# Compressed keys of the samples as weighted scores of raw pages, with page numbers kept in registers

## The reference

```python
past_cmp = kv_pool[page_table, :, 0:2].reshape(bsz, PAST_LEN, 2, NSA_KV_HEADS, NSA_HEAD_DIM)
kc, vc = nsa_compress(cmp_rows, pos_w)      # blocks of 64 rows, weighted by softmax(pos_w)
...
s_c = einsum('btkrd,bnkd->btkrn', q, kc) - slope * dist_c
p_c = masked_softmax(s_c, dist_c >= 0)
o_c = einsum('btkrn,bnkd->btkrd', p_c, vc)
imp = p_c.sum(axis=3)                       # picks the blocks of the selected branch
```

## Time and profile before

| | us |
|---|---|
| median of 3 runs | 1043.51 (1043.34 to 1045.84) |
| the profiled execution, its own time | 1046.67 |
| its span, first to last instruction | 1044.6 |
| busy in the span: TensorE, VectorE, ScalarE, GpSimd | 992.2, 492.4, 333.9, 186.0 |
| mean granted TensorE clock | 0.977 |
| loaded and stored | 343.20 MB, mean 329 GB/s |

### The profile page before, as it was taken

The page is one execution under the profiler, slowest core; times in us unless marked ns, Lnnn a source line. Parts: engine busy times, 40 slices in busy tenths (PEclk is TensorE's granted clock), DMA queues, the critical chain, the costliest instruction groups (busy, mean ns, idle before and its releaser), DMA issues. The chain is left out here.

```text
span 1044.6 us, 14969 instructions
## 1 busy us (share of the span) xinstructions
PE 992.2 (95%) x5181; PEld 618.9 (59%) x5181; DVE 492.4 (47%) x1422; ACT 333.9 (32%) x875; POOL 186.0 (18%) x201
## 2 busy tenths in 40 slices
PE   8999999899999999998999987979999999999897
PEld 6888776788744444443678864545874444444365
DVE  2889898771521111110479996671152111111056
ACT  3212888720451111110341013672045111112034
POOL 0000016321130000000345541441103000000033
PEclk9999999999999999999999995999999999999999
DMA  9963788669779999999827995959976999999974
GB/s 324 314 220 115 230 265 274 245 213 405 305 286 424 428 426 426 425 427 427 330 99 276 392 341 166 314 174 366 428 332 253 426 426 427 424 428 426 426 301 207
DMA packets 90144, 343.20 MB, mean 329 GB/s; under 512 B 15890, under 2 KB 53906, under 8 KB 73170
## 3 DMA queue, kind: packets, MB, share of 16 engines
q1 hardware_dynamic: 80074, 319.48, 78.8%
q10 hardware_dynamic: 7688, 18.39, 5.0%
q0 software_dynamic: 2304, 4.33, 1.2%
HBM read 331.56 MB, written 23.04 MB: 339 GB/s over the span
## 5 line engine op out<-in xcount | busy, mean ns | idle before, releaser
L1528 DVE TENSOR_TENSOR gates_and_hidden<-bank,gates_and_hidden 128x512 f32<-128x512 f32 x16 | 11.1, 692 | 310.6 <-PE bank L1179 310.6
L1179 PE MATMUL bank<-expert_ring,x_packed 128*64 128x512 f32 x320 | 118.3, 606 | 0.0
L1160 PE MATMUL bank<-expert_ring,x_packed 128*64 128x512 f32 x416 | 112.9, 593 | 1.1 <-DMA expert_ring<-in_moe_w_gate 0.8
L559 PE MATMUL ss<-xT,expert_ring 128*128 128x264 f32 x384 | 89.3, 392 | 4.7 <-DMA expert_ring<-in_ssd_w_in 4.7
L559 PEld LDWEIGHTS ss<-xT,expert_ring 128*128 128x128 f32 x384 | 72.9, 192 | 18.4 <-DMA xT<-in_xT 4.1
L1160 PEld LDWEIGHTS bank<-expert_ring,x_packed 128*64 128x64 f32 x416 | 36.8, 137 | 73.6 <-issue 73.6
L1389 POOL DMA_INDIRECT x_rows_packed<-x_rows,slot_token_int x16 | 16.3, 1020 | 334.8 <-DVE gates_and_hidden L1493 288.5
L1771 PE MATMUL bank<-xT,expert_ring 128*128 128x264 f32 (+1 forms) x324 | 72.7, 387 | 0.3 <-PEq L1006 0.3
L1523 DVE TENSOR_TENSOR acc<-acc,bank 128x264 f32<-128x264 f32 x128 | 54.9, 429 | 37.0 <-PE bank L1216 35.2
L1201 PE MATMUL bank<-expert_ring,gates_and_hidden 128*64 128x512 f32 x256 | 70.9, 596 | 1.4 <-ACT gates_and_hidden L1350 1.4
L1771 PEld LDWEIGHTS bank<-xT,expert_ring 128*128 128x128 f32 (+1 forms) x324 | 60.3, 187 | 12.7 <-issue 1.0
(11 more groups left out here) (419 smaller groups left out, 1829.3 us busy)
## 6 DMA issues: line engine op xcount, KB each, us to landing
expert_ring<-in_moe_w_gate SPq DMA_DIRECT2D x26, 2048.0 KB, 20.0
expert_ring<-in_moe_w_up SPq DMA_DIRECT2D x18, 2048.0 KB, 21.1
expert_ring<-in_moe_w_down SPq DMA_DIRECT2D x16, 2048.0 KB, 19.9
expert_ring<-in_ssd_w_in SPq DMA_DIRECT2D x9, 2048.0 KB, 9.1
expert_ring_b<-in_moe_w_gate SPq DMA_DIRECT2D x6, 2048.0 KB, 17.6
expert_ring_c<-in_moe_w_up SPq DMA_DIRECT2D x6, 2048.0 KB, 22.4
expert_ring_d<-in_moe_w_up SPq DMA_DIRECT2D x6, 2048.0 KB, 20.9
expert_ring_c<-in_moe_w_down SPq DMA_DIRECT2D x6, 2048.0 KB, 22.6
```

The lines of the kernel that those rows point to most:

```text
L559: last = mm(pt[m % 4][:, 0:T], wc[:, k, ((m - 1) % 4) * P:((m - 1) % 4 + 1) * P], xT[:, k, :], start=k == 0, stop=k == KD - 1)
L1160: last = mm(hb[0][s * CAP:(s + 1) * CAP, :], xg[:, k, s * CAP:(s + 1) * CAP], unit(6 * i + s)[:, k * FF:(k + 1) * FF], start=k == 0, stop= ...
L1179: last = mm(hb[1][s * CAP:(s + 1) * CAP, :], xg[:, k, s * CAP:(s + 1) * CAP], unit(6 * i + 2 + s)[:, k * FF:(k + 1) * FF], start=k == 0, s ...
```

## The change

- VectorE compresses only the values' pages: two quarters a batch, from `vcmp_pages`. GpSimd multiplies nothing there.
- The keys of the compressed branch are loaded raw beside those of the selected branch (`k_pages`). `dec_keys` has eight steps instead of four: each multiplies the samples' queries with two pages of both kinds, into two PSUM banks. VectorE then weights the raw compressed scores with the position weights and sums blocks of 64 (`key_half`), with an exponential of its own row of weights on ScalarE; the small key step has 2 columns instead of 18.
- The key steps stand between the projection's tiles 8 to 15 (`KEYS_AT`), the first prompt scores behind the gates' tile, the prompt's compressed scores two tiles later. From tile 8 on the projection alternates between two PSUM banks.
- A sixth page buffer is added (`ring_e`). One more expert unit is loaded within the block, one less at the start of `tail(1)`.
- SyncE reads the page numbers of even batches once, ScalarE those of odd ones, in the first expert stage, and they stay in registers; ScalarE issues the odd key pages between tiles (`ODD_AT`).
- Loads of bytes in all are the same but for a bias table that goes.

```diff
+        cmp_landed = lambda b: 2 * 16 * NPG * (b // 6 + 1)
...
+        even_page, odd_page = {}, {}
+        batch_pages = lambda b: range(b * NPG, (b + 1) * NPG)
...
-                        load_unit(sp, L, 3 + 2 * L, unit(3 + 2 * L))
+                        if L == 0:
+                            load_unit(sp, L, 3, unit(3))
                         load_unit(sp, L, 8, unit(8))
...
-                            page = [page_number(sp, n) for n in range(2 * NPG)]
+                            for b in range(0, DB, 2):
+                                even_page.update((n, page_number(sp, n)) for n in batch_pages(b))
+                            page = {n: page_number(sp, n) for n in batch_pages(1)}
...
-                            load_cmp(sp, 0, page)
+                            load_cmp(sp, 0, even_page)
+                            load_cmp(sp, 1, page)
                             sp.wait_ge(sc_done, n8 + 8 * NP2)
                             for c in range(2):
                                 load_chunk(sp, c, I["nsa_w_in"][c])
+                            page = {n: page_number(sp, n) for n in batch_pages(3)}
                             sp.wait_ge(e_done, 4)
-                            load_cmp(sp, 1, page)
+                            load_cmp(sp, 2, even_page)
+                            load_cmp(sp, 3, page)
...
+                                if L == 0 and 1 <= i <= DB // 2:
+                                    odd_page.update((n, page_number(act, n)) for n in batch_pages(2 * i - 1))
...
-            KV_SLOT = (1, 2, 0, 3, 4, 1, 2, 0, 3, 4, 1, 2)
+            KV_SLOT = (5, 0, 1, 2, 5, 0, 1, 2, 5, 0, 1, 2, 4, 3, 5, 0)
+            NKEY, KWIN, VAL = 8, 8, 10
...
+            GATES, nchunk = KD + 8, (KD + KVT) // 4
+            ODD_AT = {3: ((1, 0),), 4: ((1, 1),), 8: ((3, 0),), 9: ((3, 1),), 11: ((5, 0),), 12: ((5, 1),), 13: ((7, 0),), 14: ((7, 1),)}
+            KEYS_AT = {8: (0, 1), 9: (2,), 10: (3,), 12: (4,), 13: (5,), 14: (6,), 15: (7,)}
+            KV_TILE = (K_CMP, K_CMP + 1, V_CMP, V_CMP + 1, K_SEL, K_SEL + 1, K_WIN, K_WIN + 1, V_SEL, V_SEL + 1, V_WIN, V_WIN + 1)
+            tile_bank = lambda m: m if m < KD else 2 + m % 2
...
+                    load_cmp(sp, 4, even_page)
+                    sp.wait_ge(c_used, 1)
+                    load_cmp(sp, 6, even_page)
+                    name_pages(0, even_page)
+                    load_kv(sp, 0)
...
+                    name_pages(2, even_page)
                     sp.wait_ge(c_used, 6)
+                    load_kv(sp, 2)
+                    for j in range(4, NKEY, 2):
+                        name_pages(j, even_page)
+                        sp.wait_ge(kv_used, j - 3)
+                        load_kv(sp, j)
...
+                    sp.wait_ge(kv_used, VAL + 1)
+                    sp.dma_start(kv_buf[1], I["nsa_w_out"][0]).then_inc(ld_wo[0], 16)
+                    sp.wait_ge(kv_used, VAL + 2)
+                    load_unit(sp, 1, 7, kv_buf[2])
+                    sp.wait_ge(kv_used, VAL + 3)
                     load_unit(sp, 1, 0, kv_buf[4])
+                    sp.wait_ge(kv_used, VAL + 5)
+                    sp.dma_start(kv_buf[5], I["nsa_w_out"][1]).then_inc(ld_wo[1], 16)
+                    load_unit(sp, 1, 5, kv_buf[3])
+                    sp.wait_ge(kv_used, VAL + 6)
+                    load_unit(sp, 1, 3, kv_buf[0])
...
-                    for b in range(1, DB):
-                        pool.wait_ge(ld_cmp[cmp_slot(b)], 16 * NPG * (b // 3 + 1))
-                        for a in range(2, 4):
-                            cmp_multiply(nc.gpsimd, b, a).then_inc(c_mult, 1)
...
-                        if m >= 8:
-                            pe.wait_ge(tile_taken, t0 + m - 7)
+                        if m >= KD:
+                            pe.wait_ge(tile_taken, t0 + m - 1)
...
-                        k5 = kv_buf[s].rearrange("p (g q c t) -> p g q c t", g=4, q=4, c=2)
-                        for p in range(2):
-                            for g in range(4):
-                                q0 = (2 * g + t) * P + 32 * g
-                                last = mm(dp[a][32 * g:32 * g + 32, :], qbd[:, p, q0:q0 + 32], k5[:, g, :, p, :], start=t == 0 and p == 0, stop=t == 1 and p == 1)
+                        k5 = kv_buf[s].rearrange("p (g q c t) -> p g q c t", g=4, q=2, c=4)
+                        for kind, bk in enumerate((pt[4 + a], dp[a])):
+                            for p in range(2):
+                                for g in range(4):
+                                    q0 = (2 * g + t) * P + 32 * g
+                                    last = mm(bk[32 * g:32 * g + 32, pp * 256:(pp + 1) * 256], qbd[:, p, q0:q0 + 32], k5[:, g, :, 2 * kind + p, :],
+                                              start=t == 0 and p == 0, stop=t == 1 and p == 1, skip_group_check=True)
                         last.then_inc(kv_used, 1)
...
+                    for m in range(NT):
+                        tile(m)
+                        for j in KEYS_AT.get(m, ()):
+                            dec_keys(j)
+                        if m == GATES:
+                            score(0)
+                        elif m == GATES + 2:
+                            cmp_scores()
+                            turn_gates()
                     score(1)
+                    turn_new_values()
+                    turn_cmp_prompt()
...
-                        if pair <= 2:
-                            dec_keys(pair)
-                        if pair == 4:
-                            dec_keys(3)
...
+                    load_cmp(act, 5, odd_page)
+                    act.wait_ge(c_used, 2)
+                    load_cmp(act, 7, odd_page)
                     for m in range(NT):
-                        if m in (4, 8, 12):
-                            load_batch({4: 3, 8: 5, 12: 7}[m])
+                        for j, part in ODD_AT.get(m, ()):
+                            if part == 0:
+                                name_pages(j, odd_page)
+                                if j < 4:
+                                    act.wait_ge(c_used, 2 * j + 2)
+                                else:
+                                    act.wait_ge(kv_used, j - 3)
+                            load_kv(act, j, slice(4 * part, 4 * part + 4))
+                        if m == KD + 1:
+                            act.wait_ge(row_max, 1)
+                            A_(pos_row[:], pos_row[:], ACT.Exp, bias=pos_stat[:, 0:1], accum_out=pos_stat[:, 1:2]).then_inc(row_exp, 1)
...
                     exps(0)
                     exps(1)
+                    for q in range(QT):
+                        act.wait_ge(pre_tr, q + 2)
+                        A_(vtok[:, q, :], pt[2 + q][:], ACT.Copy).then_inc(vtok_ok, 1)
+                    act.wait_ge(pre_tr, 4)
+                    A_(vnew[:], dp[1][0:DB, :], ACT.Copy).then_inc(vnew_ok, 1)
...
+                        dve.wait_ge(ld_cmp[b % 6 // 2], cmp_landed(b))
                         cmp_multiply(V, b, 0)
                         dve_step(dve, cmp_multiply(V, b, 1))
                         cmp_sum(V, kcd, b, 0)
-                        cmp_sum(V, kcd, b, 1)
-                        dve.wait_ge(c_mult, 2 * b)
-                        cmp_sum(V, kcd, b, 2)
-                        cmp_sum(V, kcd, b, 3).then_inc(c_used, 1)
+                        cmp_sum(V, kcd, b, 1).then_inc(c_used, 1)
...
+                    def key_half(a):
+                        dve.wait_ge(kv_used, 4 * a + 4)
+                        raw = sw[:, 0:512].rearrange("p (n l) -> p n l", l=BLK)
+                        V.tensor_tensor(raw, pt[4 + a][:].rearrange("p (n l) -> p n l", l=BLK), pos_row[:].unsqueeze(1).to_broadcast([P, NBP // 2, BLK]), ALU.mult).then_inc(kc_read, 1)
+                        dve.wait_ge(kc_read, a + 1)
+                        dve_step(dve, V.tensor_reduce(kc_sum[:, a * NBP // 2:(a + 1) * NBP // 2], raw, AX.X, ALU.add))
+
+                    def take_half(a):
+                        V.tensor_tensor(ss[:, a * 512:(a + 1) * 512], dp[a][:], biasd[:, a * 512:(a + 1) * 512], ALU.add).then_inc(s_half, 1)
...
+                    for b in range(DB):
                         compress(b)
+                    spread_queries()
+                    dve.wait_ge(ld_nc, 16 * 12)
+                    V.tensor_reduce(pos_stat[:, 0:1], pos_row[:], AX.X, ALU.max, negate=True).then_inc(row_max, 1)
+                    dve.wait_ge(row_exp, 1)
+                    dve_step(dve, V.reciprocal(pos_stat[:, 1:2], pos_stat[:, 1:2]))
+                    key_half(0)
+                    prompt_blocks()
+                    take_half(0)
+                    key_half(1)
+                    take_half(1)
...
-                        dve_step(dve, V.tensor_tensor(sc[:], dp[0][:, 2:2 + NBP], cbd[:], ALU.add))
+                        dve_step(dve, V.scalar_tensor_tensor(sc[:], kc_sum[:], pos_stat[:, 1:2], cbd[:], ALU.mult, ALU.add))
```

356 lines of the change are left out of this document (159 added, 197 removed).

## The result

The changed kernel takes 1070.01 us, median of 4 runs (1068.33 to 1071.07), against 1044.67 (1043.34 to 1048.2) for the kernel before: a ratio of 1.0221, 95% interval 1.0189 to 1.0252. The forecast was 1047.8, range 1038.5 to 1052.0. The sign was right; the size was some six times too small.

| place (us of the profiled execution) | before | forecast | after |
|---|---|---|---|
| start of the block | 545.29 | 545.3 | 544.65 |
| first key step | - | 583.9 | 584.31 |
| end of the last tile | 618.0 | 646.8 | 662.92 |
| scores of pair 2 | 654.94 | 663.1 | 681.66 |
| first product of the output projection | 731.62 | 737.0 | 757.83 |

A forecast was written before the change was run, and what follows sets the result against it. TensorE's time from the attention block's start to the first expert product was taken as the bound. Terms +8.2 - 2.8 + 1.0 - 2.1 = +4.3 us on the median 1043.51 gave 1047.8 us, range 1038.5 to 1052.0.

The forecast's parts named there:

- the compression and its end: VectorE at the attention block's start: eight batches of 4.65 us, with the queries in their buffer at 583.9.
- The sign named for this: Ahead of the first key step: TensorE idle about 9 us, with that wait naming VectorE.
- a key step's length: TensorE's key products: 1.9 us a step, 15.2 us for eight, 7.5 us of work added.
- It doesn't do what it says: Rival at the key steps: key loads land too late and TensorE waits at each; given no chance of its own.
- the term on compression: VectorE's compression batches: 4.65 us each, 37.2 us for eight, their page loads costed at nothing.
- the drawn loop: TensorE from 583.9 to the last tile: keys, twelve tiles and small steps take 63.0 us, ending at 646.8.
- the clock: TensorE's clock falling after stands in the attention block: between 0 and 2.1 us, taken as +1.0 us.
- the stretch from the last tile to pair 2: Last projection tile to pair 2's prompt-head scores: 16.3 us, with 9.4 us of products, putting pair 2 8.2 us later.
- the loop of pairs: Prompt-head pairs from pair 2: two key steps leave, saving 3.8 us if TensorE paces, 1.9 if VectorE; taken -2.8.
- the token rows: Start of the last stage: one load fewer lets the gather follow the write sooner, -2.1 us, possibly 2.9.
- The rule on table loads: ScalarE's table switches, now three: priced at 1.28 us; by the skill's 2.66 the estimate would be 1049.2.

The follow-up runs named there:

- fill run: The changed kernel with useless products added where TensorE stands, ahead of key steps 2 and 5 and between last tile and pair 2: 1.0179 of the kernel before.
- best order: The changed kernel with key steps from tile 11 on, softmax among the tiles, odd pages asked for earlier, VectorE's compressed probabilities earlier: 0.9939 of the kernel before.

## Why the prediction was wrong

**Right: the compression and its end.** 4.65 us a batch, queries spread at 583.35 (forecast 583.9), first key step at 584.31. TensorE stood 7.34 us ahead of tile 8, and tile 8 ran at half clock, but the queries would not have let the key step begin before 583.35. The sign named for this, a wait of some 9 us on VectorE, did not come: TensorE went from tile 8 to the key step without a break, and the weights, not the queries, set its start, by 1 us. The time of this step is right in part by luck.

**Right: a key step's length**, 1.93 us at full clock.

**Wrong: the loads.** The step that failed is the rival "It doesn't do what it says", dismissed with "Every one is issued well ahead by the order, and a page landed in a median of 2.5 us before, so I give this nothing of its own", and, in the term on compression, page loads costed "at nothing". The first half of the sentence was true of step 2 (18.2 us before TensorE was ready) and less so of step 5 (6.7 us for its last page); the second is the row of a quieter stretch, and as many bytes had 22 us more there. The rows that the prediction itself showed had a DMA share of 1.01 at 621, and I did not add up the bytes due by then. At the 386 GB/s of that row the 28.66 MB that the trace counts up to step 5 take 74 us, from 547 to 621, where the drawn loop reaches step 5 at 611.4: by this estimate some 10 us of wait. From the first key step to the last tile's end it is 78.6 us instead of 63.0: 10.9 of waits for pages, 1.7 for step 5 at half clock, 1.7 for the last two tiles at low clock, and 1.3 for the rest. The runs with half the bytes, with more bytes in either kernel and with step 5 first show the cause.

**Wrong in size: the clock.** "Between 0 and 2.1 I take +1.0": it fell in four places, at 572, 620, 656 and 668. The fill run gives back 4.4 us.

**Right at full clock: the stretch from the last tile to pair 2**, drawn as 16.3 us; 18.7 in the change, 15.8 with the stands filled. The 18.5 us by which pair 2 came later than forecast are thus 16.1 up to the last tile and 2.4 behind it.

**Wrong: the loop of pairs, -2.8.** From pair 2 to the output projection it is 76.2 us against 76.7 before, so -0.5. Pairs 2 to 4 took 12.1 us against 12.77, at half clock until 684; in the best order, at full clock, they take 11.1, near the end of the range that VectorE paces (-1.9).

**Right in size, wrong in cause: the token rows, -2.1.** ScalarE's last write of rows and GpSimd's gather in the changed kernel:

```profile
801.85 0.52 ACTq L1322 DMA_DIRECT2D x_rows<-y_slots  x1
...
806.13 1.09 POOL L1404 DMA_INDIRECT x_rows_packed<-x_rows,slot_token_int  x1 [21.79 <-DVE slot_token_int L1500]
```

The gather comes 4.28 us behind the write, the first product 10.2 us, where the kernel before took 13.15, so 3.0 us are won, at the outer bound. I had put that down to the second load at the stage's start; with that load back in its place the run shows 4.29. The likely cause is that the backlog of weights behind it ends earlier against the write; that was read from the traces, not tried by itself.

**The rule on table loads.** ScalarE's timeline behind the last tile:

```profile
663.02 0.39 ACT L2063 ACTIVATE expert_ring_c<-bank 128x264 f32<-128x264 f32 x1 [3.17 <-PE bank L1802]
...
663.43 1.28 ACT L2073 ACT_TABLE_LOAD   x1
...
664.73 0.40 ACT L2073 ACTIVATE gates_and_hidden<-gates_and_hidden,neg_max 128x128 f32<-128x128 f32 x1
```

The load takes 1.28 us and the exponentials begin 0.02 us after it, with the take of the tile ended 0.02 us before. So the whole switch costs 1.3 us here. The Trainium skill (ScalarE: Activation LUTs, "What ACT_TABLE_LOAD costs") gives about 2.66 with a drain; this trace does not agree.

What the traces say of key pages from two queues: in the changed kernel from 570 us on, those asked for by SP took 7.8 us (16 pages) and 11.1 (the 8 of the sixth buffer) in the median, those by ScalarE 10.4, and asking earlier for step 5's only made step 7 wait. The Trainium skill (DMA: Bandwidth & Descriptors, "Issuing engines are not separate DMA queues") says that transfers of all issuing engines share the same DMA engines and interleave; this trace agrees.

## What to carry to other kernels

Where a change brings work forward, add up the bytes due by the new time and divide by the rate that the stretch shows: a transfer hidden before is priced by its due time, not by its latency in a quieter stretch. If the sum doesn't fit, place other work between the steps that need the bytes and ask for them in the order in which they are due; together with a softmax drawn in among the tiles, that turned +2.2% into -0.6% here, with the same bytes and the same products. Undo suspected causes one at a time even where a term came out right: the token rows were won for another reason than the one given.

## What the runs showed of the hardware

The granted clock fell while TensorE was busy all the time: behind the prompt's compressed scores, 16 products of 8 columns (32 records) in one run of 3.9 us, it was 0.61 in the stretch at 628 of the best order, and the next tile took 5.31 us instead of 3.83. With the same products in two runs of 1.95 us, a tile between, it stayed at 1.00. The long run of very small products so cost 1.5 us here; half clock behind the stand ahead of step 5 cost 1.7.

Pages of 256 KB moved at 386 GB/s with the DMA engines full, weights of 2 MB at 428. A copy from HBM to HBM held SP's queue 0.49 us an issue (0.69 with what stands between two), a load of a page 0.33 in the median, and up to 4.0 with the extra copies ahead of it.
